# A fused three-layer block on one core: reordering the preparation of keys and values ahead of the attention heads

## The reference, cut to what matters

```python
a = rmsnorm(h, mix_norm[i])
u = a @ w_in[i]
(qa, kc, vc, ksl, vsl, kwn, vwn, ga, qf, kf, vf, fl) = jnp.split(u, split_points, axis=-1)
q_a = partial_rope(rmsnorm(split_heads(qa, N_HEADS_NSA), q_norm_nsa[i]), cos, sin)
kc_tok = partial_rope(split_heads(kc, N_KV_NSA), cos, sin)
k_cmp = rmsnorm(compress_blocks(kc_tok, cmp_pos_k[i], cmp_k_w1[i], cmp_k_w2[i]), k_norm_cmp[i])
v_cmp = compress_blocks(split_heads(vc, N_KV_NSA), cmp_pos_v[i], cmp_v_w1[i], cmp_v_w2[i])
k_slc = partial_rope(rmsnorm(split_heads(ksl, N_KV_NSA), k_norm_slc[i]), cos, sin)
k_win = partial_rope(rmsnorm(split_heads(kwn, N_KV_NSA), k_norm_win[i]), cos, sin)
gates = jax.nn.sigmoid(ga).reshape(b, s, N_HEADS_NSA, 3).transpose(0, 2, 1, 3)
```

## Time and profile before

| | us |
|---|---|
| median of 3 runs | 2895.47 |
| lowest and highest | 2891.57, 2895.85 |
| profiled execution | 2895.47 |
| its span in the profile | 2893.6 |
| TensorE busy | 2759.3 (95%) |
| VectorE busy | 1360.4 (47%) |
| ScalarE busy | 1013.0 (35%) |

### The profile page before, as it was taken

One profiled execution on the slowest core, in us unless ns is written; L12 is line 12 of the kernel. 1 busy time (PEld: TensorE's weight loads), 2 busy tenths in 40 slices (PEclk: granted clock), 3 DMA queues, 4 the chain that ended last, 5 costly groups with the idle time before them and its releaser, 6 DMA issues.

```text
span 2893.6 us, 46447 instructions
## 1 busy us (share of the span) xinstructions
PE 2759.3 (95%) x19096; PEld 2007.4 (69%) x19096; DVE 1360.4 (47%) x2285; ACT 1013.0 (35%) x1570; POOL 300.0 (10%) x250
## 2 busy tenths in 40 slices
PE   7999998899999989989999999999999899999999
PEld 3566666468888634678888778888465567788886
DVE  6566566253333257663333444433244776344335
ACT  5334333144332223644432332222011574232223
POOL 3232323010000002310000010000000131000000
PEclk9999999999999999999999999999999999999999
DMA  5334333222232111022232122232021002222331
GB/s 223 108 125 137 131 124 119 102 88 101 90 117 86 61 52 51 10 94 96 92 112 100 64 73 101 91 111 106 32 102 58 1 9 78 90 101 87 114 111 59
DMA packets 46292, 261.07 MB, mean 90 GB/s; under 512 B 5128, under 2 KB 7576, under 8 KB 26168
## 3 DMA queue, kind: packets, MB, share of 16 engines
q1 hardware_dynamic: 45128, 254.23, 25.0%
q10 hardware_dynamic: 1008, 4.57, 0.4%
HBM read 256.63 MB, written 2.15 MB: 89 GB/s over the span
## 4 chain that ended last, share of the span: by engine, by line
PE 89%; DVE 4%; ACT 3%; POOL 1%; issue 1%; DMA 1%; SPq 0%; DVEq 0%; ACTq 0%; POOLq 0%; PEld 0%; PEldq 0%
PE psum L214 87%; PE psum L2064 2%; DMA ada_first<-in_ada_first 1%; POOL branch_in L564 1%; POOL ysum L562 0%; DVE residual L1539 0%; ACT L608 0%; POOL join L557 0%; DVE residual L1531 0%; ACT yg L642 0%; DVE Y_pairs L770 0%; ACT ln_in L1494 0%; ACT nsa_probs L2100 0%; DVE ln_stat L1523 0%; DMA weights<-in_cmp_w 0%
## 5 line engine op out<-in xcount | busy, mean ns | idle before, releaser
L1657 ACT ACTIVATE ffn_weights_hi<-weights 128x1024 fp32r<-128x1024 f32 (+1 forms) x128 | 145.9, 1142 | 490.7 <-PE psum L214 490.7
L214 PE MATMUL psum<-ffn_in_hi,ffn_weights_hi 128*128 128x512 f32 x768 | 304.8, 397 | 12.4 <-DVE ffn_weights_lo L1660 7.8
L214 PE MATMUL psum<-ffn_in_hi,ffn_weights_lo 128*128 128x512 f32 x768 | 301.8, 393 | 0.0
L214 PE MATMUL psum<-ffn_in_lo,ffn_weights_hi 128*128 128x512 f32 x768 | 301.8, 393 | 0.0
L1657 ACT ACTIVATE ff_weights_hi<-weights 128x1024 fp32r<-128x1024 f32 (+1 forms) x120 | 137.7, 1147 | 433.4 <-PE psum L214 433.4
L214 PE MATMUL psum<-ff_in_hi,ff_weights_hi 128*128 128x512 f32 x704 | 277.4, 394 | 11.5 <-DVE ff_in_lo L1545 7.2
L214 PE MATMUL psum<-ff_in_lo,ff_weights_hi 128*128 128x512 f32 x704 | 276.5, 393 | 0.0
L214 PE MATMUL psum<-ff_in_hi,ff_weights_lo 128*128 128x512 f32 x704 | 276.2, 392 | 0.0
L1660 DVE TENSOR_TENSOR ff_weights_lo<-weights,ff_weights_hi 128x1024 fp32r<-128x1024 f32 (+1 forms) x116 | 156.2, 1347 | 253.5 <-ACT ff_weights_hi L1657 253.5
L1660 DVE TENSOR_TENSOR ffn_weights_lo<-weights,ffn_weights_hi 128x1024 fp32r<-128x1024 f32 (+1 forms) x126 | 166.9, 1326 | 110.5 <-ACT ffn_weights_hi L1657 110.5
L214 PEld LDWEIGHTS psum<-ffn_in_hi,ffn_weights_hi 128*128 128x128 f32 x768 | 146.2, 190 | 47.5 <-DVE ffn_weights_lo L1660 9.1
(11 more groups left out here) (519 smaller groups left out, 4878.4 us busy)
## 6 DMA issues: line engine op xcount, KB each, us to landing
weights<-in_ff_in SPq DMA_DIRECT2D x44, 1024.0 KB, 4.7
weights<-in_ffn_in SPq DMA_DIRECT2D x44, 1024.0 KB, 4.7
weights<-in_ada SPq DMA_DIRECT2D x80, 512.0 KB, 3.5
weights<-in_ff_out SPq DMA_DIRECT2D x16, 1408.0 KB, 6.0
weights<-in_ffn_out SPq DMA_DIRECT2D x16, 1408.0 KB, 6.0
weights<-in_rwkv SPq DMA_DIRECT2D x8, 1152.0 KB, 5.6
weights<-in_fox_qkv SPq DMA_DIRECT2D x4, 1536.0 KB, 6.4
weights<-in_rwkv SPq DMA_DIRECT2D x8, 640.0 KB, 4.0
```

The costliest lines, as they stand in the source:

```text
L214: return nc.tensor.matmul(out, lhsT, rhs, start=start, stop=stop)
L1657: return nc.scalar.activation(sp_.hi[u][:, 0:width], slot[s][:, u * width:(u + 1) * width], ACT.Copy)
```

## The change

The order of work in `mixer_inputs` is changed, and the first transfers of `head_inputs`. No product, vector operation or transfer is added or removed.

- TensorE: "win" and "vals" follow directly on "fl". Then come "kc rot", "slc sum", "win sum", "v twice", "k twice", "slc rot", "win rot", and then the four cmp products without anything between. The products "cmp0" and "cmp1" now wait for "win sin" too.
- VectorE: the copies of the values come directly behind "z"; then kc, the norms of "slc" and "win", the blocks of v, the blocks of k, and the turning of "slc" and "win".
- ScalarE: the squares of "win" come before the square root of "slc".
- SyncE: the first transfers of the heads' weights move into the loop, which runs from 0; both wait ahead of the loop for the last use of both slots, "cmp2" and "cmp3".

```diff
-            PE = ["kc", "vc", "slc", "gates", "fl", "kc rot", "slc sum", "win", "k twice", "slc rot", "win sum", "vals", "win rot", "cmp0",
-                  "v twice", "cmp1", "cmp2", "cmp3", "k2", "v2", "k2 sum"]
-            AC = ["slc sq", "kc", "vc", "gates", "slc std", "win sq", "win std", "abs", "exp", "ln",
+            PE = (["kc", "vc", "slc", "gates", "fl", "win", "vals", "kc rot", "slc sum", "win sum", "v twice", "k twice", "slc rot",
+                   "win rot"] + [f"cmp{n}" for n in range(loads_n)] + ["k2", "v2", "k2 sum"])
+            AC = ["slc sq", "kc", "vc", "gates", "win sq", "slc std", "win std", "abs", "exp", "ln",
...
-            DV = (["z", "kc cos", "kc sin", "kc", "slc rstd", "slc n"] + [f"blocks k{g}{r}{n}" for g in range(2) for r in range(2) for n in range(2)]
-                  + ["win rstd", "win n", "vals0", "vals1"] + [f"{n} {m}" for n in ("slc", "win") for m in ("cos", "sin", "add")]
-                  + [f"blocks v{g}{r}{n}" for g in range(2) for r in range(2) for n in range(2)]
+            DV = (["z", "vals0", "vals1", "kc cos", "kc sin", "kc"] + [f"{n} {m}" for n in ("slc", "win") for m in ("rstd", "n")]
+                  + [f"blocks {u}{g}{r}{n}" for u in "vk" for g in range(2) for r in range(2) for n in range(2)] + [f"{n} {m}" for n in ("slc", "win") for m in ("cos", "sin", "add")]
...
+                for u, ready, banks in (("v", (act_done, "vc"), (6, 7)), ("k", (dve_done, "kc"), (0, 1))):
+                    pe.wait_ge(*reached(*ready))
+                    if u == "v":
+                        pe.wait_ge(*dve_done("vals1"))
+                    for g in range(2):
+                        last = mm(ps[:, banks[g], :], cc(f"twice{g}"), toks[:, "kv".index(u), :])
+                    last.then_inc(*pe_done.step(f"{u} twice"))
+                for n, (name, bank) in enumerate((("slc", 2), ("win", 5))):
+                    pe.wait_ge(*dve_done(f"{name} n"))
+                    mm(ps[:, bank, :], cc("rot"), raw[:, n, :]).then_inc(*pe_done.step(f"{name} rot"))
 
                 pe.wait_ge(*act_done("win std"))
                 for n, l in enumerate(cmp_loads):
                     u, part = n // 2, n % 2
                     pe.wait_ge(*dve_done(f"blocks {'kv'[u]}111"))
-                    if u:
-                        pe.wait_ge(*dve_done("win sin"))
+                    pe.wait_ge(*dve_done("win sin"))
                     pe.wait_ge(*l.arrived())
...
-                    if n == 0:
-                        pe.wait_ge(*dve_done("vals1"))
-                        twice("v", (6, 7))
...
             def sp(sp):
-                for load, stream in ((n_load, "nsa_q"), (f_load, "fox_qkv")):
-                    sp.wait_ge(*load.vacated())
-                    sp.dma_start(load.slot(row(stream, 0)), row(stream, 0)).then_inc(*load.arrival)
-                with sp.Fori(1, N) as i:
+                sp.wait_ge(*n_load.vacated())
+                sp.wait_ge(*f_load.vacated())
+                with sp.Fori(0, N) as i:
                     for load, stream in ((n_load, "nsa_q"), (f_load, "fox_qkv")):
                         sp.wait_ge(*load.vacated(i))
                         sp.dma_start(load.slot(row(stream, i)), row(stream, i)).then_inc(*load.arrival)
```

More of the change, by code:

```diff
@@ L2566, in pe @@
                 last.then_inc(*pe_done.step("fl"))
[L2567 to L2572, removed]
                 pe.wait_ge(*load_b.arrived())
@@ L2576, in pe @@
                 last.then_inc(*pe_done.step("win"))
[L2578 to L2586, removed]
                 for q in range(QT):
[L2588 to L2591, removed]
                     for k in range(KT):
@@ L2595, in pe @@
                 last.then_inc(*pe_done.step("vals"))
-                pe.wait_ge(*dve_done("win n"))
-                mm(ps[:, 5, :], cc("rot"), raw[:, 1, :]).then_inc(*pe_done.step("win rot"))
+                pe.wait_ge(att_in, 48)
+                pe.wait_ge(*act_done("kc"))
+                mm(ps[:, 0, :], cc("rot"), raw[:, 2, :]).then_inc(*pe_done.step("kc rot"))
+                for n, (name, bank, free) in enumerate((("slc", 3, (act_done, "gates")), ("win", 4, (dve_done, "z")))):
+                    pe.wait_ge(*act_done(f"{name} sq"))
+                    pe.wait_ge(*reached(*free))
+                    mm(ps[:, bank, :], blockones, sq[:, n, :]).then_inc(*pe_done.step(f"{name} sum"))
+                for u, ready, banks in (("v", (act_done, "vc"), (6, 7)), ("k", (dve_done, "kc"), (0, 1))):
[8 more added lines that the diff above has]
+                    mm(ps[:, bank, :], cc("rot"), raw[:, n, :]).then_inc(*pe_done.step(f"{name} rot"))
                 pe.wait_ge(*act_done("win std"))
@@ L2639, in act @@
                 a(gates[:, :, :], ps[:, 3, 0:QT * 24].rearrange("p (q n) -> p q n", n=24), ACT.Sigmoid).then_inc(*act_done.step("gates"))
+                act.wait_ge(*pe_done("win"))
+                a(sq[:, 1, :], ps[:, 5, :], ACT.Square).then_inc(*act_done.step("win sq"))
                 for n, (name, bank) in enumerate((("slc", 3), ("win", 4))):
-                    if n:
-                        act.wait_ge(*pe_done("win"))
-                        a(sq[:, 1, :], ps[:, 5, :], ACT.Square).then_inc(*act_done.step("win sq"))
                     act.wait_ge(*pe_done(f"{name} sum"))
@@ L2672, in dve @@
                 ts(z[:, 0, :], ps[0:8, 4, :], vcol("b_forget")[0:8, :], None, ALU.add).then_inc(*dve_done.step("z"))
-                def normed(n, name, bank):
+                dve.wait_ge(*pe_done("vals"))
+                for b in range(2):
+                    nc.vector.tensor_copy(vals[:, 2 * b:2 * b + 2, :], ps[:, 6 + b, :].rearrange("p (q n) -> p q n", q=2)).then_inc(*dve_done.step(f"vals{b}"))
+                dve.wait_ge(att_in, 48)
+                dve.wait_ge(*act_done("kc"))
+                tt(cos[:, :], raw[:, 2, :], cc("cos"), ALU.mult).then_inc(*dve_done.step("kc cos"))
+                dve.wait_ge(*pe_done("kc rot"))
+                tt(sin[:, 2, :], ps[:, 0, :], cc("sin"), ALU.mult).then_inc(*dve_done.step("kc sin"))
+                dve.wait_ge(*dve_done("kc sin"))
+                tt(toks[:, 0, :], cos[:, :], sin[:, 2, :], ALU.add).then_inc(*dve_done.step("kc"))
+                for n, (name, bank) in enumerate((("slc", 2), ("win", 5))):
                     dve.wait_ge(*act_done(f"{name} std"))
@@ L2678, in normed @@
                     stt(raw[:, n, :], ps[:, bank, :], vcol(f"k_{name}"), rstd[:, n, :], ALU.mult, ALU.mult).then_inc(*dve_done.step(f"{name} n"))
-                def made_blocks(u, banks):
+                for u, banks in (("v", (6, 7)), ("k", (0, 1))):
                     dve.wait_ge(*pe_done(f"{u} twice"))
@@ L2692, in made_blocks @@
                                    ALU.add).then_inc(*dve_done.step(f"blocks {u}{g}{r}{later}"))
[L2693 to L2705, removed]
                 for n, (name, bank) in enumerate((("slc", 2), ("win", 5))):
@@ L2712, in dve @@
                     tt(keys[name][:, :], keys[name][:, :], sin[:, n, :], ALU.add).then_inc(*dve_done.step(f"{name} add"))
-                made_blocks("v", (6, 7))
                 dve.wait_ge(*act_done("exp"))
```

## The result

The changed kernel takes 2915.93 us (median of four runs, 2913.86 to 2918.57) where the kernel before takes 2894.33 (four runs, 2891.57 to 2895.85). These medians lie 21.6 us apart. The ratio on record, which also takes in eleven further runs of the changed kernel (all fifteen: 2913.86 to 2926.92 us), is 1.0088 with a 95% interval of 1.0074 to 1.0102, so it is slower, by 21 to 30 us. The forecast was 2919.3 us in a range of 2907 to 2923.

A forecast was written before the change was run, and what follows sets the result against it. TensorE, busy for 2759.3 of 2893.6 us, was taken as the bound. The terms 15.06 − 1.77 − 1.43 + 11.61 + 0.3 gave 23.8 us on 2895.5, hence 2919.3 us, range 2907 to 2923.

The forecast's parts named there:

- VectorE's chain: Behind the vals products VectorE works 20.9 us in one piece, from the copies of vals to win sin.
- start of cmp0: The first cmp product waits for win sin and starts at about 2120.4 instead of 2105.34: 15.06 us later.
- v twice moved away: The v twice product leaves the cmp part: 1.77 us less.
- idle time for the weight row: TensorE's wait for the last row of compression weights goes away: 1.43 us less.
- four cmp products: All four run at half clock, 7.04 us a product, 28.16 us together: 11.61 us more.
- in_nsa_q: The heads' first query row, asked for behind cmp3, lands just past the old start: 0.3 us more.
- Early part: On TensorE, moving win and vals ahead of the rotation and the sums costs nothing.
- Half clock throughout: The clock stays at half speed through all four cmp products; likeliest case, 2919 us, chance 0.62.
- Rivals one: Full clock returns while the cmp products run: +14.4 + 0.3 us, or 2910 us; chance 0.18.
- Rival two: The clock never drops, so cmp0 runs at full speed: +11.1 + 0.3 us, or 2906.9 us; chance 0.07.
- Rival three: SyncE's loop entry costs two us, colder first query products one or two more: 2923 us; chance 0.08.
- rivals four and five: Four: VectorE's chain doesn't bind, weight-row wait and clock fall go, 2889 us, 0.02. Five: later slack absorbs it, no change, 0.03.

The follow-up runs named there:

- the filled kernel: Changed kernel with 13 extra 512-column products, results unread, in TensorE's idle times ahead of slc rot, win rot and cmp0; ratio to before 1.0067.
- the wide burst: Changed kernel with six extra 512-column products, results unread, between cmp0 and cmp1; one run, 2921.37 us.
- k2 early: Kernel before with k2 and k2 sum between cmp2 and cmp3, and their square and square root ahead of ScalarE's silu of v; ratio 0.9989.

## Why the prediction was right

The measured stage against the terms of the sum, counted from the start of "fl":

| term | predicted | measured |
|---|---|---|
| VectorE's chain, copies to win sin | 20.9 | 20.75 (2097.53 to 2118.28) |
| start of cmp0 | +15.06 | +15.35 (50.33 against 34.98) |
| v twice moved away | −1.77 | −1.77 |
| idle time for the weight row | −1.43 | −1.43 |
| four cmp products | +11.61 (28.16) | +10.92 (2118.70 to 2146.17 is 27.47) |
| in_nsa_q | +0.3 | +0.87 |
| sum | 23.8 | 23.94 |

**Early part.** "win" and "vals" in front cost nothing, as said.

**VectorE's chain.** The order and each duration came out within 0.2 us. The idle times were 1.35, 2.92 and 7.73 us against 1.6, 3.1 and 8.5. The last is shorter than forecast since "win rot" itself ran at half clock, 2.08 us. The run with the blocks of k first shows the chain as the cause: 6 us less of it ahead of "cmp0" starts "cmp0" 6.8 us sooner.

**Half clock throughout.** A product took 6.87 us instead of 7.04, which I had taken as twice the 3.52 at full clock, so this term came out 0.7 us too high. This was the step with the widest range, 11.1 to 23.5 us, and the upper end held. The choice of the row behind idle time over the row at full clock was right. (The 19.5 matmuls that the prediction works out for that row don't fit its own count of 22; the trace has 0.215 us a matmul at half clock, 27.47 / 128.) The runs now show more than the prediction could: filled idle times give full clock, and wide products in the middle bring it back. What I had taken as the reason, that narrow products don't lift the clock, was seen again over 27.47 us without a pause. Rivals one (the clock comes back by itself) and two (it never falls) are out. Rival two's price, 11.1 + 0.3 us, is near the +11.3 of the kernel with all idle times filled, but by chance: that kernel has twenty extra products, and its query products run at full clock (14.00 us against 16.57). Rival two as worked out, however, would not have happened even on a full clock at "cmp0", since the wait for weight row 2 brings it down.

By the Trainium skill ("TensorE: Matmul & The Clock Gate", "What's actually happening") the clock comes back after sustained busy activity, without a condition on width. Here 27.47 us of back-to-back 62-column products stayed at 0.50, so the measurement decides. The same page of the Trainium skill ("HAM oscillation — how this bites in real kernels") puts the fall down to waits between groups of products; that agrees in kind with the 1.55 us wait between "cmp1" and "cmp2" of the filled kernel. The fall inside the unbroken "gates" product isn't of that kind.

**SyncE.** The term was mis-sized: 0.87 instead of 0.3. The landing took 3.56 us, under the 3.9 I used, but the request left 1.20 us behind "cmp3" (2147.37 − 2146.17), where I had 0.1 to 0.4. The run with SyncE's part alone has the same 1.19, and with the old part a transfer behind the same step leaves after 0.10. How the 1.1 us divide between the waits and the loop's entry was not measured. Rival three is out: it had 2 us for the entry and one or two more for colder heads, but the first query products take 16.57 us against 16.59.

**Opposite side and no change.** VectorE's chain binds, and the span behind the stage is 748.1 us in both kernels, so rivals four and five are out. In the profiled pair the stages ahead of the change were 2.0 us quicker, and the predicted 2919.3 lies 2.0 us above that execution's 2917.28. The sum itself, 23.8 us on the stage, was met within 0.2, and that close a match is luck: the cmp term was 0.7 too high, and the start of "cmp0" and SyncE's term were 0.3 and 0.6 too low.

## What to carry to other kernels

An order that alternates one engine's long products with small ones for another engine's sake was worth more here than tidy groups: moving the wide products ahead left VectorE idle for 20 us and then TensorE waiting for VectorE. A wait in front of a stretch of small products can cost more than its length, as the whole stretch may run at half clock; price such stretches at both levels, and ask for every wait inside them. Where a short wait can't be removed, move other work into it, and measure a throwaway product there as a test of what the clock costs.

## What was not expected of the hardware

A stretch of 62-column float32 products kept whichever level it was given: 0.50 for 27.47 us in the changed kernel, 1.00 for over 7 us behind the wide burst. Products of 24 columns didn't: the clock fell inside "gates" with TensorE busy all the time. Idle times shorter than expected end the full clock in a stretch of 62-column products: 1.43 us was enough in the kernel before. With k2 early the clock fell behind two of only 0.31 and 0.40 us, with 31-column products before and between them. Four products whose results are thrown away made the kernel before quicker by 0.25% (0.16 to 0.34%).
